# Warm-up multiplications, a first weight half in two pieces, and query tile before key tile in a two-layer block kernel

## The chip, the cores and the metric

One core of a Trainium2 chip runs the whole program. The metric is the device time in microseconds (us), the median of three runs. Engines: TensorE (PE; PEld is its weight load), VectorE (DVE), ScalarE (ACT), GpSimd (POOL), SyncE (SP, here only a queue that issues transfers).

## The reference, cut to what matters

A sequence of 256 tokens of width 1024 goes through two layers. Each layer normalises the tokens, multiplies them by the wide `w_in` and mixes them in four branches; the attention branch needs normalised queries and keys:

```python
xn = rms_norm(h, norm1_g[layer])
z = xn @ w_in[layer]
q, k, va = jnp.split(z[..., OFF_ATTN:OFF_GATE], 3, axis=-1)
q = rms_norm(q, q_g)                      # over 64 features, 8 groups
k = rms_norm(k, k_g)
bias = rel_bias[rel_buckets(qp, kp)]
logits = einsum('bhmqd,bhmkd->bhmqk', qb, kb) * scale + bias
```

Behind the mixing follow a dense feed-forward part in layer 0 and eight experts in layer 1, then a second block of two layers with other mixers. The change touches only the start of the program and the query and key part of both layers of the first block.

## The kernel before

Every product of a float32 activation with a float32 weight is made of three: high by high, low by high and high by low part, where high is the value rounded to the short format and low what is left. ACT makes the high part of a weight half (`split`, line 1672, 128x2048) and DVE the low part (line 2194). `weigh` takes the halves of a tile in turn: per half and token block it issues 4 x 2 matmuls with the high weights (alternating xT_high and xT_low) and then 4 with the low weights, all on line 917. A tile of 1024 x 512 (Q, K, V and so on) has two halves, so 24 matmuls for each of the two token blocks, 48 in all.

**Loads.** SP issues x block 0, x block 1 and then all weight halves in order of use (lines 838, 839, 836): Q, K and V have two halves of 1 MB each. Five raw slots hold halves, so the first five loads (Q both, K both, V first) wait for nothing; V's second half takes the slot of Q's first half and is asked for once PE has used it for both blocks. POOL issues 26 loads of constants; its large ones (line 1550, 2.8 MB with the masks in first_constants) wait until Q's second half is in.

**Token blocks.** Each block of 128 tokens is normalised (ACT line 1636 for the squares, lines 1626 and 1627 for the root, DVE line 2179), turned by 8 transposes on PE (`norm_turn`, line 964), and copied by ACT to xT_high (line 1643) and by DVE to xT_low (line 2187).

**Order on PE** in `mixer`: Q block 0, transposes of x block 1, K block 0, Q block 1, K block 1, each by `by_block`. In layer 0 the transposes of x block 0 come first; in layer 1 they come earlier, and the splits of Q and K lie in the feed-forward part before. Then come VEC (a small product for the bias, layer 0 only), SW (transposes of the gating weights), QT (transposes of the normalised queries, two blocks), V, KT (of the keys), UV with its two results U and SV, in layer 0 FLIP (line 1035), and A.

**Order on ACT and DVE.** Both run fixed lists. For the norm of each of Q and K, block by block: ACT squares the result (`head_squares`, line 1731), DVE sums (`head_sums`, line 2267), ACT takes the root in two steps (`head_roots`, lines 1626 and 1627), DVE multiplies (`head_norm`, line 2274). Between these steps lie the splits of V and UV. Behind them DVE copies VEC (line 2293), prepares parameters (line 2246 on) and masks SW (line 2302). POOL writes the copied VEC to DRAM (line 1554), reads it back shifted (line 1556) as `brev`, and PE waits for that before FLIP.

**Banks.** Results take eight PSUM banks in turn, in the order of `first_jobs`; `begin` waits until the job that had the bank eight jobs before has been drained. In layer 0 U has the bank of VEC and SV that of SW; in layer 1 U has that of K block 1 and SV that of SW. `weigh` asks for all banks of its jobs before its first matmul.

Of the kernel before, what the change touches and what calls it, by code (L numbers as in the profile page):

```python
# [60 lines left out]
NHIGH = 3  # L61

# [164 lines left out]
def first_jobs(l):  # L227
    j = norm_jobs("1", l, blocks=(0,)) if l == 0 else []
    j += [("Q", l, 0)] + norm_jobs("1", l, blocks=(1,)) + [("K", l, 0), ("Q", l, 1), ("K", l, 1)]
# [135 lines left out]
def kernel_program(nc, t):  # L365
# [28 lines left out]
    with ctx:  # L394
# [3 lines left out]
        def sem(name):  # L398
            return ctx.enter_context(nc.semaphore(name))
# [122 lines left out]
        lgt = A(2, 2, SEQ)  # L522
        prb = A(2, 2, SEQ)
# [123 lines left out]
        x_in, ident_in, first_in = sem("x_in"), sem("ident_in"), sem("first_in")  # L647
# [11 lines left out]
        rt_weights, rt_mask = sem("rt_weights"), sem("rt_mask")  # L659
        hn_y_out, index_ready, rows_fetched = sem("hn_y_out"), sem("index_ready"), sem("rows_fetched")  # L660
        sel_ready, f_sel_ready, moe_done, f_done = sem("sel_ready"), sem("f_sel_ready"), sem("moe_done"), sem("f_done")
        flag_ready, router_high_in = sem("flag_ready"), sem("router_high_in")
# [158 lines left out]
        def _(sp):  # L821
# [16 lines left out]
            sp.dma_start(h[:, 0, :], t["x"][0, 0:P, :]).then_inc(x_in, 16)  # L838
            sp.dma_start(h[:, 1, :], t["x"][0, P:SEQ, :]).then_inc(x1_in_out_done, 16)
            for half in DENSE[:FIRST_HALVES]:  # L840
                load_half(half)
# [39 lines left out]
        def _(pe):  # L881
# [121 lines left out]

            def mixer(l):
                if l == 0:
                    pe.wait_ge(ident_in, 16)
                    norm_turn(("1", l), 0, xs, (norm_x, 1))
                pe.wait_ge(*drained(("X", "1", l, 0, 1)))
                by_block(("Q", l), ("Q", l), 0)
                norm_turn(("1", l), 1, xs, (norm_x, 4 * l + 2))  # L1010
                by_block(("K", l), ("K", l), 0)
                pe.wait_ge(*drained(("X", "1", l, 1, 1)))
                by_block(("Q", l), ("Q", l), 1)
                by_block(("K", l), ("K", l), 1)
# [6 lines left out]
                def heads(name, src, first):  # L1021
                    for b in range(TB):
                        pe.wait_ge(qk_n, at(l, 4, 2 * b + first + 1))
# [261 lines left out]
            pe.wait_ge(rt_mask, 1)  # L1285
# [329 lines left out]
        def _(act):  # L1615
            steps = Steps(act, act_step)
            act.dma_start(norm1_row, t["norm1_g"][0].partition_broadcast(P)).then_inc(norm1_row_in[0], 16)
            act.dma_start(ident, t["common_constants"][:, 0:P]).then_inc(ident_in, 16)
# [99 lines left out]
            def mixer(l):  # L1718
                if l == 0:
                    log_exp()  # L1720
                    norm(0, (x_in, 16))
                    norm(1, (x1_in_out_done, 16))
                    high("1", l, 0)
                    split(("Q", l))
                    split(("K", l))
                    high("1", l, 1)
# [6 lines left out]
                def head_roots(n, b):  # L1733
                    k = 2 * n + b
                    act.wait_ge(qk_ss, at(l, 4, 2 * b + n + 1))
                    inv_root(tiny[:, 8 * k:8 * k + 8], tiny[:, 8 * k:8 * k + 8], QK, qk_r)
                head_squares(0, 0)
                head_squares(1, 0)
                head_roots(0, 0)
# [1325 lines left out]
```

## Time and profile before

| | |
|---|---|
| median of 3 runs | 2178.29 us (2177.87 to 2179.69) |
| the profiled execution | 2178.79 us, its span 2176.6 us |
| PE busy | 2137.2 us, 98% of the span, 10935 matmuls |
| DVE, ACT busy | 1591.8 us (73%), 1331.9 us (61%) |
| PE, share of the chain that ended last | 90%; DVE 4%, transfers 3%, ACT 2% |

The span runs from the first to the last instruction; the execution is 2.2 us longer. In a timeline a line gives the start, the duration, the engine and source line, the operation, how many were merged (x8), and, where the engine sat idle before, how long and which operation ended it. Matmuls overlap, so their spacing is less than the duration shown.

### The profile page before, as it was taken

What the parts mean: (1) busy time and instruction counts of PE and PEld (TensorE: products, weight loads), DVE (VectorE), ACT (ScalarE), POOL (GpSimd) and SP (SyncE); (2) the same over time, 40 slices, a digit from 0 to 9 for tenths busy, and PEclk for the clock granted to TensorE, in tenths of its full rate; (3) what the DMA queues carried; (4) which work ended last, traced back from release to release, by engine and by line L of the source; (5) the groups of instructions that cost most, each with busy time, mean ns of one, the idle gap of its engine ahead of it and who ended that gap; (6) DMA issues with size and microseconds to landing.
All of it is one profiled execution on the core that took longest, in us unless ns stands there. A gap on an engine that the chain in (4) does not pass through costs nothing.

```text
span 2176.6 us, 27831 instructions
## 1 busy us (share of the span) xinstructions
PE 2137.2 (98%) x10935; PEld 1811.7 (83%) x10935; DVE 1591.8 (73%) x1339; ACT 1331.9 (61%) x1151; POOL 78.2 (4%) x67
## 2 busy tenths in 40 slices
PE   7999999999998999999999999999999999999998
PEld 5988788888787888888888888888888898899987
DVE  5577555466766888888888889888896667565665
ACT  4475544355655777777777777777765545456542
POOL 3100000000000000000000000000110000000000
PEclk9999999999998999999999999999999999999999
DMA  8554565554548999999999999999996534455442
GB/s 281 157 190 150 206 199 184 178 187 149 194 153 294 351 373 380 375 380 375 389 370 386 379 378 373 383 382 373 388 368 218 174 124 148 163 179 170 132 155 78
DMA packets 249165, 569.70 MB, mean 262 GB/s; under 512 B 12168, under 2 KB 14352, under 8 KB 248816
## 3 DMA queue, kind: packets, MB, share of 16 engines
q1 hardware_dynamic: 242368, 546.41, 70.3%
q0 software_dynamic: 5136, 16.70, 2.3%
q10 hardware_dynamic: 1568, 5.31, 0.6%
q8 instruction: 64, 1.05, 0.2%
q14 instruction: 29, 0.24, 0.0%
HBM read 562.60 MB, written 5.78 MB: 261 GB/s over the span
## 4 chain that ended last, share of the span: by engine, by line
PE 90%; DVE 4%; DMA 3%; ACT 2%; issue 0%; SPq 0%; DVEq 0%; ACTq 0%
PE bank L917 33%; PE bank L1178 9%; PE bank L1179 9%; PE bank L1182 9%; PE bank L923 9%; PE bank L1226 5%; PE bank L1219 5%; PE bank L1221 5%; PE bank L964 3%; DMA ring<-w_in 2%; DVE halves_r L2194 1%; DMA ring<-moe_w_down 1%; ACT halves_r L1672 1%; DVE w_low L2622 0%; DMA ring<-w_out 0%
## 5 line engine op out<-in xcount | busy, mean ns | idle before, releaser
L2622 DVE TENSOR_TENSOR w_low<-ring,w_high 128x4096 fp32r<-128x4096 f32 x167 | 736.4, 4421 | 80.5 <-ACT w_high L1901 80.2
L1901 ACT ACTIVATE w_high<-ring 128x4096 fp32r<-128x4096 f32 x167 | 607.1, 3636 | 232.8 <-DMA ring<-moe_w_gate_up 137.0
L917 PE MATMUL bank<-halves_r,xT_high 128*128 128x512 f32 (+1 forms) x1856 | 562.6, 381 | 5.9 <-ACT halves_r L1672 3.2
L2194 DVE TENSOR_TENSOR halves_r<-ring,halves_r 128x2048 fp32r<-128x2048 f32 x175 | 391.4, 2264 | 160.9 <-ACT halves_r L1672 159.0
L917 PEld LDWEIGHTS bank<-halves_r,xT_high 128*128 128x128 f32 x1856 | 343.8, 189 | 73.1 <-issue 5.2
L1672 ACT ACTIVATE halves_r<-ring 128x2048 fp32r<-128x2048 f32 x175 | 326.2, 1892 | 118.6 <-DMA ring<-w_in 57.4
L1178 PE MATMUL bank<-w_high,xg_high 128*128 128x512 f32 x896 | 354.7, 396 | 1.7 <-DVE xg_low L2599 1.7
L1179 PE MATMUL bank<-w_high,xg_low 128*128 128x512 f32 x896 | 349.6, 390 | 0.0
L917 PE MATMUL bank<-halves_r,xT_low 128*128 128x512 f32 (+1 forms) x928 | 348.5, 380 | 0.0
L1182 PE MATMUL bank<-w_low,xg_high 128*128 128x512 f32 x896 | 221.6, 389 | 0.0
L917 PEld LDWEIGHTS bank<-halves_r,xT_low 128*128 128x128 f32 x928 | 175.3, 189 | 31.7
L1178 PEld LDWEIGHTS bank<-w_high,xg_high 128*128 128x128 f32 x896 | 168.4, 188 | 35.9 <-issue 1.9
L1182 PEld LDWEIGHTS bank<-w_low,xg_high 128*128 128x128 f32 x896 | 168.1, 188 | 35.1 <-DVE w_low L2622 0.2
L1179 PEld LDWEIGHTS bank<-w_high,xg_low 128*128 128x128 f32 x896 | 168.4, 188 | 33.8
L1219 PE MATMUL bank<-w_high,hid_high 128*128 128x512 f32 x448 | 176.5, 394 | 0.0
L1221 PE MATMUL bank<-w_high,hid_low 128*128 128x512 f32 x448 | 174.5, 390 | 0.0
L923 PE MATMUL bank<-xT_high,halves_r 128*128 128x256 f32 x896 | 165.2, 284 | 0.0
L1650 ACT ACTIVATE arena<-bank 128x512 f32<-128x512 f32 x82 | 47.4, 597 | 158.1 <-PE bank L923 82.8
L923 PEld LDWEIGHTS bank<-xT_high,halves_r 128*128 128x128 f32 x896 | 141.0, 192 | 0.9 <-issue 0.8
L1226 PE MATMUL bank<-w_low,hid_high 128*128 128x512 f32 x448 | 112.2, 389 | 0.6 <-DVE w_low L2622 0.6
L923 PE MATMUL bank<-xT_low,halves_r 128*128 128x256 f32 x448 | 108.8, 283 | 0.0
L1219 PEld LDWEIGHTS bank<-w_high,hid_high 128*128 128x128 f32 x448 | 84.1, 188 | 19.2 <-ACT w_high L1901 2.0
(392 smaller groups left out, 2310.9 us busy)
## 6 DMA issues: line engine op xcount, KB each, us to landing
ring<-moe_w_gate_up SPq DMA_DIRECT2D x224, 1024.0 KB, 10.6
ring<-moe_w_down SPq DMA_DIRECT2D x112, 1024.0 KB, 9.8
ring<-w_in SPq DMA_DIRECT2D x108, 1024.0 KB, 5.1
ring<-w_out SPq DMA_DIRECT2D x24, 1024.0 KB, 4.9
ring<-ffn_w_gate_up SPq DMA_DIRECT2D x22, 1024.0 KB, 5.2
ring<-ffn_w_down SPq DMA_DIRECT2D x11, 1024.0 KB, 4.9
ring<-w_mem_kv SPq DMA_DIRECT2D x8, 1024.0 KB, 5.2
ring<-w_branch_attn SPq DMA_DIRECT2D x4, 1024.0 KB, 5.1
```

What stands on the lines that cost most here:

```text
L917: return pe.matmul(o[:, a:a + n], x[:, c, b * P:(b + 1) * P], w[:, k, col:col + n], **flags)
L923: return pe.matmul(o[:, a:a + SEQ], w[:, k, j * P:(j + 1) * P], x[:, c, :], **flags)
L1178: pe.matmul(o[:, :], xg_high[:, c, :], w[:, c, :], start=c == 0, stop=False)
L1179: pe.matmul(o[:, :], xg_low[:, c, :], w[:, c, :], start=False, stop=False)
L1182: mm = pe.matmul(o[:, :], xg_high[:, c, :], w[:, c, :], start=False, stop=c == KC - 1)
L1219: pe.matmul(acc[n][:, :], hid_high[:, 4 * k + c, :], v[:, c, :], start=k + c == 0, stop=False)
L1221: pe.matmul(acc[n][:, :], hid_low[:, 4 * k + c, :], v[:, c, :], start=False, stop=False)
L1226: mm = pe.matmul(acc[n][:, :], hid_high[:, 4 * k + c, :], v[:, c, :], start=False, stop=4 * k + c == EX_CH - 1)
L1672: act.activation(top_view(half), raw_view(half), ACT.Copy).then_inc(top_in, 1)
L1901: act.activation(high_slot(k), ring[:, ring_r.slot(names[k]), :], ACT.Copy).then_inc(w_high_in[r], 1)
L2194: dve.tensor_tensor(raw_view(half, halves_r), raw_view(half), top_view(half).bitcast(F32), ALU.subtract).then_inc(raw_low_in, 1)
L2622: dve.tensor_tensor(w_low[:, slot, :], ring[:, slot, :], high_slot(k).bitcast(F32), ALU.subtract).then_inc(w_low_in[r], 1)
```

## The change

- SP loads Q's first half in two pieces of two chunks each: the first piece between x block 0 and x block 1, the second behind x block 1. ACT and DVE make its high and low parts piece by piece.
- DVE sets 640 columns to zero at the very start, and PE multiplies them 20 times (512 columns each) into a bank that nobody reads, before it waits for the identity matrix and the first piece, whose arrival the same semaphore now tells.
- In layer 0 `first_queries` replaces the block-wise order: Q's chunks 0 and 1 for block 0, chunks 2 and 3, the transposes of x block 1, the low part for block 0, the near half for block 1, then the far half for both blocks.
- In both layers the order is Q block 0, transposes, Q block 1, and then K for both blocks joined, half by half (in layer 0 behind `first_queries`). ACT's and DVE's lists are put in that order, root and norm directly behind their squares and sums; the two splits of UV now stand together behind the last root and norm.
- Some semaphores are shared by two uses (renamed, with higher counts).

The diff, cut to its core:

```diff
+WARM_UP = 20
...
-    j += [("Q", l, 0)] + norm_jobs("1", l, blocks=(1,)) + [("K", l, 0), ("Q", l, 1), ("K", l, 1)]
+    j += [("Q", l, 0)] + norm_jobs("1", l, blocks=(1,)) + [("Q", l, 1), ("K", l, 0), ("K", l, 1)]
...
+        zeros_r = rounded("zeros_r", [P + WIDE], arena_at + 4 * A.at)
...
+            first, first_from = raw_view(DENSE[0]), dense_source(*DENSE[0])
+            sp.dma_start(first[:, 0:2, :], first_from[:, 0:2, :]).then_inc(ident_piece_in, 16)
             sp.dma_start(h[:, 1, :], t["x"][0, P:SEQ, :]).then_inc(x1_in_out_done, 16)
-            for half in DENSE[:FIRST_HALVES]:
+            sp.dma_start(first[:, 2:4, :], first_from[:, 2:4, :]).then_inc(raw_full[raws.slot(DENSE[0])], 16)
+            for half in DENSE[1:FIRST_HALVES]:
...
+            def first_queries():
+
+                tile = ("Q", 0)
+                near, far = (tile, 0), (tile, 1)
+                out = {0: begin((*tile, 0))}
+
+                def high(b, w, c, k):
+                    rows(b)(out[b], xT_high, w, c, k, start=c == 0, stop=False)
+                    return rows(b)(out[b], xT_low, w, c, k, start=False, stop=False)
+
+                def low(b, w, c, k):
+                    return rows(b)(out[b], xT_high, w, c, k, start=False, stop=c == KC - 1)
+
+                pe.wait_ge(*drained(("X", "1", 0, 0, 0)))
+                pe.wait_ge(piece_top_router_high, 1)
+                for c in (0, 1):
+                    high(0, top_view(near), c, c)
+                w = high_half(near)
+                for c in (2, 3):
+                    high(0, w, c, c)
+                norm_turn(("1", 0), 1, xs, (norm_x, 2))
+                w_low = low_half(near)
+                for c in range(4):
+                    low(0, w_low, c, c)
+                out[1] = begin((*tile, 1))
+                pe.wait_ge(*drained(("X", "1", 0, 1, 0)))
+                for c in range(4):
+                    mm = high(1, w, c, c)
+                mm.then_inc(top_free[tops.slot(near)], 1)
+                for c in range(4):
+                    mm = low(1, w_low, c, c)
+                mm.then_inc(*raw_end(near))
+                pe.wait_ge(*drained(("X", "1", 0, 0, 1)))
+                pe.wait_ge(*drained(("X", "1", 0, 1, 1)))
+                w = high_half(far)
+                for b in range(TB):
+                    for k in range(4):
+                        mm = high(b, w, 4 + k, k)
+                mm.then_inc(top_free[tops.slot(far)], 1)
+                w_low = low_half(far)
+                for b in range(TB):
+                    for k in range(4):
+                        mm = low(b, w_low, 4 + k, k)
+                    mm.then_inc(*end((*tile, b)))
+
             def mixer(l):
                 if l == 0:
-                    pe.wait_ge(ident_in, 16)
+                    pe.wait_ge(zeros_rt_mask, 1)
+                    for k in range(WARM_UP):
+                        pe.matmul(bank[NBANK - 1][:, :], zeros_r[:, 0:P], zeros_r[:, P:P + WIDE], start=True, stop=True)
+                    pe.wait_ge(ident_piece_in, 32)
                     norm_turn(("1", l), 0, xs, (norm_x, 1))
-                pe.wait_ge(*drained(("X", "1", l, 0, 1)))
-                by_block(("Q", l), ("Q", l), 0)
-                norm_turn(("1", l), 1, xs, (norm_x, 4 * l + 2))
-                by_block(("K", l), ("K", l), 0)
-                pe.wait_ge(*drained(("X", "1", l, 1, 1)))
-                by_block(("Q", l), ("Q", l), 1)
-                by_block(("K", l), ("K", l), 1)
+                    first_queries()
+                else:
+                    pe.wait_ge(*drained(("X", "1", l, 0, 1)))
+                    by_block(("Q", l), ("Q", l), 0)
+                    norm_turn(("1", l), 1, xs, (norm_x, 4 * l + 2))
+                    pe.wait_ge(*drained(("X", "1", l, 1, 1)))
+                    by_block(("Q", l), ("Q", l), 1)
+                weigh(("K", l), [(("K", l, b), [rows(b)]) for b in range(TB)])
                 pe.wait_ge(first_in, FIRST_LOADS * 16)
                 if l == 0:
                     pe.matmul(begin(("VEC",))[0:MAPS, 0:REL], rel_tab, rel_hot, start=True,
...
-                        pe.wait_ge(qk_n, at(l, 4, 2 * b + first + 1))
+                        pe.wait_ge(qk_n, at(l, 4, 2 * first + b + 1))
...
                 if l == 0:
                     log_exp()
                     norm(0, (x_in, 16))
+                    first, first_top = raw_view(DENSE[0]), top_view(DENSE[0])
+                    act.wait_ge(ident_piece_in, 32)
+                    act.activation(first_top[:, 0:2, :], first[:, 0:2, :], ACT.Copy).then_inc(piece_top_router_high, 1)
+                    high("1", l, 0)
                     norm(1, (x1_in_out_done, 16))
-                    high("1", l, 0)
-                    split(("Q", l))
+                    act.wait_ge(raw_full[raws.slot(DENSE[0])], 16)
+                    act.activation(first_top[:, 2:4, :], first[:, 2:4, :], ACT.Copy).then_inc(top_in, 1)
+                    high("1", l, 1)
+                    split(("Q", l), (1,))
                     split(("K", l))
-                    high("1", l, 1)

                 def head_squares(n, b):
                     job = ("QK"[n], l, b)
...
-                    act.wait_ge(qk_ss, at(l, 4, 2 * b + n + 1))
+                    act.wait_ge(qk_ss, at(l, 4, k + 1))
                     inv_root(tiny[:, 8 * k:8 * k + 8], tiny[:, 8 * k:8 * k + 8], QK, qk_r)
                 head_squares(0, 0)
+                head_roots(0, 0)
+                head_squares(0, 1)
+                head_roots(0, 1)
+                split(("V", l), (0,))
                 head_squares(1, 0)
-                head_roots(0, 0)
                 head_roots(1, 0)
-                split(("V", l), (0,))
-                head_squares(0, 1)
                 split(("V", l), (1,))
-                head_roots(0, 1)
                 head_squares(1, 1)
-                split(("UV", l), (0,))
                 head_roots(1, 1)
-                split(("UV", l), (1,))
+                split(("UV", l))
                 act.wait_ge(first_in, 16 * FIRST_LOADS)
                 act.wait_ge(par_exp, 2 * l + 1)
                 act.activation(small[:, l, 16:18], small[:, l, 14:16], ACT.Exp).then_inc(par_exp, 1)
...

             def mixer(l):
                 if l == 0:
+                    dve.memset(zeros_r[:, :].bitcast(F32), 0.0).then_inc(zeros_rt_mask, 1)
+                    first, first_top, first_low = raw_view(DENSE[0]), top_view(DENSE[0]), raw_view(DENSE[0], halves_r)
                     dve.wait_ge(norm1_row_in[0], 16)
-                    for b in range(TB):
-                        norm(b, b + 1, norm1_row)
+                    norm(0, 1, norm1_row)
+                    dve.wait_ge(piece_top_router_high, 1)
+                    dve.tensor_tensor(first_low[:, 0:2, :], first[:, 0:2, :], first_top[:, 0:2, :].bitcast(F32),
+                                      ALU.subtract)
                     lower("1", l, 0)
-                    split(("Q", l))
+                    norm(1, 2, norm1_row)
+                    dve.wait_ge(top_in, 1)
+                    dve.tensor_tensor(first_low[:, 2:4, :], first[:, 2:4, :], first_top[:, 2:4, :].bitcast(F32),
+                                      ALU.subtract).then_inc(raw_low_in, 1)
+                    lower("1", l, 1)
+                    split(("Q", l), (1,))
                     split(("K", l))
-                    lower("1", l, 1)

                 def head_sums(n, b):
                     k = 2 * n + b
-                    dve.wait_ge(qk_sq, at(l, 4, 2 * b + n + 1))
+                    dve.wait_ge(qk_sq, at(l, 4, k + 1))
                     dve.tensor_reduce(tiny[:, 8 * k:8 * k + 8], shaped(sq_t[:, k, :], 8, QK), AX.X,
                                       ALU.add).then_inc(qk_ss, 1)

                 def head_norm(n, b):
                     job, dst = ("QK"[n], l, b), (q_n, k_n)[n]
                     k = 2 * n + b
-                    dve.wait_ge(qk_r, at(l, 4, 2 * b + n + 1))
+                    dve.wait_ge(qk_r, at(l, 4, k + 1))
                     link(dve.tensor_tensor(shaped(dst[:, b, :], 8, QK), shaped(out_of(job)[:, :], 8, QK),
                                            over(tiny[:, 8 * k:8 * k + 8], QK), ALU.mult))
                     dve.sem_inc(qk_n, 1)
                     dve.sem_inc(*fr(job))
                 head_sums(0, 0)
+                head_norm(0, 0)
+                head_sums(0, 1)
+                head_norm(0, 1)
+                split(("V", l), (0,))
                 head_sums(1, 0)
-                head_norm(0, 0)
                 head_norm(1, 0)
-                split(("V", l), (0,))
-                head_sums(0, 1)
                 split(("V", l), (1,))
-                head_norm(0, 1)
                 head_sums(1, 1)
-                split(("UV", l), (0,))
                 head_norm(1, 1)
-                split(("UV", l), (1,))
+                split(("UV", l))
                 if l == 0:
                     dve.wait_ge(first_in, 16 * FIRST_LOADS)
                     dve.wait_ge(*full(("VEC",)))
```

## Rows read from the trace of the kernel before

**Rows 1.** Busy time by stretches: us, PE, PEld, DVE, ACT, POOL, PEclk, DMA, GB/s.

```profile
66.33:100.00 33.67, 33.67 (x259) 31.32 (x258) 18.95 (x29) 13.59 (x13) 7.26 (x10) 1.00 0.57 143
...
1644.00:1648.00 4.00, 3.79 (x21) 3.71 (x20) 0.00 (x0) 3.97 (x4) 0.00 (x0) 0.62 0.60 225
```

**Rows 2.** Timeline of ACT, layer 0: start us, us, engine, line, operation, [idle before, releaser].

```profile
6.22 1.06 ACT L1636 ACTIVATE xs<-h 128x1024 f32<-128x1024 f32 x1 [3.25 <-DMA h<-x]
...
8.35 1.06 ACT L1636 ACTIVATE xs<-h 128x1024 f32<-128x1024 f32 x1 [0.51 <-DMA h<-x]
...
12.45 1.91 ACT L1672 ACTIVATE halves_r<-ring 128x2048 fp32r<-128x2048 f32 x1 [0.50 <-DMA ring<-w_in]
16.54 1.91 ACT L1672 ACTIVATE halves_r<-ring 128x2048 fp32r<-128x2048 f32 x1 [2.19 <-DMA ring<-w_in]
...
33.20 1.92 ACT L1672 ACTIVATE halves_r<-ring 128x2048 fp32r<-128x2048 f32 x1 [2.04 <-DMA ring<-w_in]
...
43.44 0.21 ACT L1627 ACTIVATE arena<-arena 128x8 f32<-128x8 f32 x1
```

**Rows 3.** Timeline of all engines, 9 to 12 us.

```profile
9.38 1.94 PE L964 MATMUL bank<-consts,xs 128*128 128x128 f32 x8 [9.38 <-DVE xs L2179]
...
10.01 1.28 DVE L2179 SCALAR_TENSOR_TENSOR xs<-h,rstd,arena 128x1024 f32<-128x1024 f32 x1 [0.77 <-ACT rstd L1627]
...
11.21 1.47 DVE L2187 TENSOR_TENSOR xT_low<-bank,xT_high 128x512 fp32r<-128x512 f32 x2
```

**Rows 4.** Timeline of DVE, layer 0, 35 to 51 us.

```profile
35.15 2.29 DVE L2194 TENSOR_TENSOR halves_r<-ring,halves_r 128x2048 fp32r<-128x2048 f32 x1 [2.94 <-ACT halves_r L1672]
...
41.55 0.68 DVE L2274 TENSOR_TENSOR arena<-bank,arena 128x512 f32<-128x512 f32 x1
42.48 0.69 DVE L2267 TENSOR_REDUCE arena<-arena 128x8 f32<-128x512 f32 x1 [0.24 <-DVE arena L2274]
43.08 2.28 DVE L2194 TENSOR_TENSOR halves_r<-ring,halves_r 128x2048 fp32r<-128x2048 f32 x1
...
48.42 0.54 DVE L2293 COPY arena<-bank 8x384 f32<-8x384 f32 x1
...
50.57 0.69 DVE L2302 TENSOR_TENSOR arena<-bank,consts 128x512 f32<-128x512 f32 x1
```

**Rows 5.** Timelines of PE and of POOL, layer 0, 40 to 66 us.

```profile
40.43 0.81 PE L1017 MATMUL bank<-arena 32*8 32x384 f32 x2
...
54.57 0.36 PE L923 MATMUL bank<-xT_high,halves_r 128*128 128x256 f32 x1
...
66.17 1.03 PE L1035 MATMUL bank<-arena,consts 128*128 128x256 f32 x4
...
49.25 0.55 POOL L1554 DMA_DIRECT2D bias_by_distance<-arena  x1 [26.32 <-DVE arena L2293]
...
63.45 0.90 POOL L1570 DMA_DIRECT2D par_all<-mem_norm_g  x1 [8.47 <-DMA arena<-bias_by_distance]
```

**Rows 6.** Timelines of PE and of DVE, layer 1, 442 to 474 us.

```profile
442.00 1.03 PE L964 MATMUL bank<-consts,xs 128*128 128x128 f32 x8
...
461.65 0.66 PE L964 MATMUL bank<-consts,arena 128*128 128x128 f32 x4 [1.40 <-DVEq L2276]
...
473.87 0.36 PE L923 MATMUL bank<-xT_high,halves_r 128*128 128x256 f32 x1
...
443.29 1.28 DVE L2187 TENSOR_TENSOR xT_low<-bank,xT_high 128x512 fp32r<-128x512 f32 x2
...
467.98 0.15 DVE L2246 SCALAR_TENSOR_TENSOR arena<-arena 128x1 f32<-128x1 f32 x1
...
469.69 0.69 DVE L2302 TENSOR_TENSOR arena<-bank,consts 128x512 f32<-128x512 f32 x1
```

**Rows 7.** Chain of work that ended last, layer 1: start us, us, what.

```profile
462.31 10.93 PE bank L917 x48
```

**Rows 8.** Timeline of PE, behind the experts.

```profile
1642.71 0.35 PE L923 MATMUL bank<-mg_high_a,halves_r 128*128 128x256 f32 x1 [2.23 <-DVE mg_low_b L2708]
```

More of the change, by code:

```diff
@@ L646, in kernel_program @@
         f_bank_free = [sem(f"f_bank_free{k}") for k in range(NBANK)]
-        x_in, ident_in, first_in = sem("x_in"), sem("ident_in"), sem("first_in")
+        x_in, ident_piece_in, first_in = sem("x_in"), sem("ident_piece_in"), sem("first_in")
         vec_out, brev_in = sem("vec_out"), sem("brev_in")
@@ L658, in kernel_program @@
         merged_up = sem("merged_up")
-        rt_weights, rt_mask = sem("rt_weights"), sem("rt_mask")
+        rt_weights, zeros_rt_mask = sem("rt_weights"), sem("zeros_rt_mask")
         hn_y_out, index_ready, rows_fetched = sem("hn_y_out"), sem("index_ready"), sem("rows_fetched")
         sel_ready, f_sel_ready, moe_done, f_done = sem("sel_ready"), sem("f_sel_ready"), sem("moe_done"), sem("f_done")
-        flag_ready, router_high_in = sem("flag_ready"), sem("router_high_in")
+        flag_ready, piece_top_router_high = sem("flag_ready"), sem("piece_top_router_high")
         ye_high_in = {"m": sem("ye_high_in"), "f": sem("f_ye_high_in")}
@@ L1284, in _ @@
                 norm_turn(("E",), b, memS, (mem_x, b + 1))
-            pe.wait_ge(rt_mask, 1)
+            pe.wait_ge(zeros_rt_mask, 2)
             o = begin(("RK",))
@@ L1617, in _ @@
             act.dma_start(norm1_row, t["norm1_g"][0].partition_broadcast(P)).then_inc(norm1_row_in[0], 16)
-            act.dma_start(ident, t["common_constants"][:, 0:P]).then_inc(ident_in, 16)
+            act.dma_start(ident, t["common_constants"][:, 0:P]).then_inc(ident_piece_in, 16)
             def log_exp():
@@ L1958, in _ @@
             mixer(0)
-            act.activation(flat(router_high), flat(router), ACT.Copy).then_inc(router_high_in, 1)
+            act.activation(flat(router_high), flat(router), ACT.Copy).then_inc(piece_top_router_high, 1)
             ffn()
@@ L2508, in route @@
                                            over(index[:, :, k], 8), ALU.is_equal))
-                dve.tensor_tensor(chosen_r, rt[:, 72:88], rt[:, 88:104], ALU.add).then_inc(rt_mask, 1)
+                dve.tensor_tensor(chosen_r, rt[:, 72:88], rt[:, 88:104], ALU.add).then_inc(zeros_rt_mask, 1)
                 top = shaped(rt[:, 16:32], TB, 8)
@@ L2513, in route @@
                 dve.wait_ge(*full(("RK",)))
-                dve.wait_ge(rt_mask, 1)
+                dve.wait_ge(zeros_rt_mask, 2)
                 link(dve.scalar_tensor_tensor(out=pos[:, :, 0:8], in0=shaped(out_of(("RK",))[:, 0:16], TB, 8), scalar=1.0,
@@ L2695, in _ @@
             mixer(0)
-            dve.wait_ge(router_high_in, 1)
+            dve.wait_ge(piece_top_router_high, 2)
             dve.tensor_tensor(flat(router_low), flat(router), flat(router_high).bitcast(F32), ALU.subtract)
```

## The prediction

> **What bounds the kernel now.** I read three views in this order. First the page (table above): TensorE (PE) is busy 98% of the span, nearly all of it matmuls that the change keeps, so only its idle time can be won. Then the busy time by stretches: after the first 66 us PE is busy without a gap [rows 1], so whatever moves the start of the FLIP matmuls, at 66.17 us [rows 5], moves the end by as much. Then the timelines of the first 66 us, engine by engine, because all that the change touches lies there and in the same stretch of layer 1, 442 to 474 us.
>
> In the first 66 us three clocks run beside each other. The loads: x block 0 is in at 6.2, x block 1 at 8.35, the first half of the Q weights at 12.45, the second at 16.54, and the first half of V only at 33.20, because GpSimd's large constant loads start once Q's second half is in and share the transfer engines [rows 2]. PE: 8 transposes take 1.94 us at 9.38 and 1.03 at 442.00 [rows 3, 6], the two levels of 1.2 and 2.4 GHz; at the upper one 48 matmuls of 512 columns take 10.93 us, 0.228 each [rows 7]. VectorE (DVE): from 35.15 on it has one long list, low parts of V and UV, sums and norms of Q and K, the copy of VEC, the masking of SW [rows 4]. The reader should see that this list, not PE, decides what a faster start is worth.
>
> **The start: zeros, split load, first_queries.** The SP queue now holds x0, first piece, x1, second piece; the bytes are the same. x1 came 2.1 us after x0 and has 512 KB; the 1 MB of Q's first half came 4.1 after x1 [rows 2]. So the first piece is in at 8.4, x1 at 10.4, the second piece at 12.45, and what is behind keeps its time.
>
> The Trainium skill ("DMA: Bandwidth & Descriptors", Anatomy of one DMA) gives each DMA about 2 us of fixed cost beside its bytes. Paid in series by the one extra DMA it would make every later load, V's too, 2.0 us later and put the estimate 2.0 us higher. The rows speak against it: 512 KB and 1 MB arrive at the same rate, with no room for a fixed part between queued DMAs.
>
> The memset and the 20 multiplications of zeros run on engines that have nothing to do before x is in. At twice 0.228 they last at most 9.1 us, so they may hold the first transposes (9.38, rows 3) by up to 1.3 us.
> Then, with the rows' durations: ACT splits the first piece at 8.7 to 9.8 (half of a split) and copies the transposes of x0 to 11.2; norm 1 follows there and not at 8.35, so that DVE has x1's norm (1.66 from ACT's start, then 1.28, rows 2, 3) at 14.3 instead of 11.3. DVE has the piece's low part at 11.1 and the first low transpose at 11.8; there PE begins Q block 0, with 4 matmuls. It waits for the second piece's top (13.95), does 4 more, the 8 transposes of x1, 4 low ones, waits for block 1's first low transpose (17.1), does 12, and from 19.8, behind the split of Q's second half, the last 24. Q is done for both blocks at 25.3. K, joined, is 48 matmuls: 36.2, its block 0, after 44 of them, 35.3. K's loads are early enough. VEC (0.74), SW and both QT (12 transposes, 1.2), V (10.93) and KT (0.8) bring PE to UV at 49.9, where it was at 54.57 [rows 5]. If nothing else were late, the start would give 4.7 us.
>
> **What is late next.** UV's accumulators reuse the banks of VEC and SW, which DVE drains behind its whole list. VEC also feeds the bias round trip through DRAM that FLIP waits for. So DVE's list in the new order:
> - V's first half is in at 33.20 as before: its load is queued from the start, and GpSimd's loads begin when they did. Low part 35.15 to 37.4 [rows 4]. K block 0 and its squares (36.2) are not late.
> - Sum from 37.36; from its start to the end of ACT's roots were 1.17 us (42.48 to 43.65, rows 4, 2): 38.53. The norm holds DVE 0.93 (41.55 to 42.48, rows 4), to 39.5.
> - ACT's split of V's second half is now behind these roots: 38.45 to 40.35. Its load, which ended this wait before, is asked for much earlier, when Q block 1 has used the near half. Low part from 40.4; it holds DVE 2.2: 42.6.
> - Sum, roots to 43.75, norm to 44.7. ACT's split of UV, behind the roots too, ends at 45.57. Low parts of UV from 45.6 and 47.8; the VEC copy starts at 50.0.
>
> Before, it started at 48.42 [rows 4]: now 1.6 later, although PE is 4.7 earlier. The splits of UV used to fill the time in which DVE waited for the roots; now these waits are open. SW's masking starts 2.15 behind the copy and takes 0.69 [rows 4]: banks free at 52.85. PE starts UV at 52.9 and has waited 3.0 us, a wait that was not there, with everything behind it. FLIP is ready 11.6 later (54.57 to 66.17, rows 5): 64.5. The bias round trip ends at 63.45 before [rows 5]; 1.6 later, PE has it at about 64.85 (POOL sees it 0.2 late). FLIP starts at 64.85 instead of 66.17: **layer 0 gains 1.3 us** of the 4.7. Bounds: 4.7 gained, if the list is not the limit; and 1.7 lost, if the round trip, 14.2 us now [rows 5], takes a fifth longer (67.8), since 2.7 of slack are all it had.
>
> **Layer 1, where there is no start to win.** The same code orders layer 1.
> - Q block 1 now follows block 0 directly and needs x1's low transposes, which K block 0 covered. PE ends the transposes at about 442.8, DVE ends the low ones at 443.29 + 1.28 = 444.57 [rows 6]: PE loses 1.8.
> - 72 matmuls (Q block 1, K) take 16.4: SW at 461.0. The wait of 1.40 before QT block 1 [rows 6] goes, since Q's norms are long done. V starts at 462.2, against 462.1. By PE alone UV starts at 473.9, against 473.87 [rows 6]: nothing won or lost.
> - But K block 0 is done at 460.2 instead of 448. Sum from 460.9, roots 462.1, V's second half on ACT to 464.0 and on DVE to 466.15, sum and roots to 467.3, UV on ACT to 469.1, on DVE from 469.15 and 471.35 to 473.6. The parameter steps start at 473.6 instead of 467.98, SW's masking 1.71 later, and takes 0.69 [rows 6]: 476.0. PE starts UV at 476.0: **layer 1 loses 2.1 us**, with 0 (the list is quicker) and 3 as bounds.
>
> **Sum.** The profiled execution has 2178.79 us, its span 2176.6 and 2.2 around it. -1.3 + 2.1 = +0.8: 2179.6. The median of the runs is 0.5 lower: **2179.1**. That is within 0.2% (4.4 us, about what a measurement of this kernel can tell from no change).
>
> **Rivals.**
> - A: the start reaches the end. For it: PE alone is at UV at 49.9. Against it: V's first half is tied to 33.20 and the list behind it is in a fixed order. Layer 0 -4.7, layer 1 +2.1: 2175.7. If the list does not bind in layer 1 either, 2173.6, just faster by over 0.2%.
> - B: slower, through the clock. The change makes PE wait 3.0 us before UV in layer 0, 1.8 before Q block 1 and 2.1 before UV in layer 1. In the old trace a wait of 2.23 at 1642.71 [rows 8] was followed by a stretch whose granted clock is 0.62 in the mean of 4 us, the lower level most of the time [rows 1]; the wait of 1.40 [rows 6] was not. It decides between these. Price: 0.38 x 4 = 1.5 us and a little before it, 1.6. In layer 0 the first 0.35 of it is covered by the round trip. Once: 2180.5; three times: 2183.5, slower. The Trainium skill ("TensorE: Matmul & The Clock Gate", Loop structure matters more than you think) holds that matmuls behind long waits run cold; the rows at 1642.71 agree. By that rule all three new waits would cost it, and the time would be this rival's 2183.5.
> - C: the zeros don't do what they are there for: the clock falls again behind them. 12 matmuls more at 0.456 cost Q up to 2.5 us; the sum over K block 0 can start 1.2 late before DVE waits for it; 1.3 of it shows: 2180.4.
>
> **How the numbers follow.** The forecast 0.52; A 0.17 (0.05 of it at 2173.6); B 0.22 (0.08 of it slower by over 0.2%); C 0.09. The range leaves out the far ends of A and B: 2174.8 to 2183.2. Faster by over 0.2%: 0.05, slower: 0.08, within: 0.87.
>
> **What would show it.** Right: the VEC copy near 50.0, UV starting near 52.9 released by DVE, FLIP near 64.9; in layer 1 PE idle at 443 to 444.6 and before UV, not before QT block 1. Wrong: PE goes into UV without a wait (A); a clock below 1 near 53, 445 or 476 (B); transposes or matmuls at the lower level past 18 us (C); V's first half not in at 33.2, which would move all of layer 0.

## The result, and the profile after

| | before | changed |
|---|---|---|
| median, 8 runs each | 2178.60 us (2177.38 to 2181.13) | 2184.53 us (2182.47 to 2186.17) |
| ratio | | 1.0021, 95% interval 1.0012 to 1.0031 |
| the profiled execution, span | 2178.79, 2176.6 us | 2182.55, 2180.7 us |

The change costs time: 5.9 us by the medians; the ratio on record, which is not the quotient of the medians, gives 4.6 us, its interval 2.6 to 6.8. The forecast was 2179.1, made of a loss of 0.8 us, with a range to 2183.2. The median lies 1.3 above that range; by the ratio the time beside the forecast's own base (2178.29) would be 2182.9, just inside it. Three executions, 2609 us of the kernel before and 3249 and 5971 us of the kernel before with zeros, are far slower than all others and count in no ratio and in no median below.

The page of the changed kernel (busy us, share, instructions):

```profile
span 2180.7 us, 27881 instructions
## 1 busy us (share of the span) xinstructions
PE 2144.0 (98%) x10955; PEld 1816.5 (83%) x10955; DVE 1592.5 (73%) x1341; ACT 1331.2 (61%) x1152; POOL 78.2 (4%) x67
```

PE has only 20 matmuls more, the zeros, and 6.8 us more of busy time. Where the time went can be read by four milestones that both kernels have. The first two are where the change is. This is DVE's timeline in layer 0 of the changed kernel (start us, us, engine, line, operation), beside [rows 4]:

```profile
35.16 2.29 DVE L2252 TENSOR_TENSOR halves_r<-ring,halves_r 128x2048 fp32r<-128x2048 f32 x1 [3.03 <-ACT halves_r L1726]
...
38.56 0.69 DVE L2340 TENSOR_TENSOR arena<-bank,arena 128x512 f32<-128x512 f32 x1 [0.52 <-ACT arena L1681]
40.37 2.29 DVE L2252 TENSOR_TENSOR halves_r<-ring,halves_r 128x2048 fp32r<-128x2048 f32 x1 [1.11 <-ACT halves_r L1726]
42.57 0.68 DVE L2333 TENSOR_REDUCE arena<-arena 128x8 f32<-128x512 f32 x1
...
45.58 4.50 DVE L2252 TENSOR_TENSOR halves_r<-ring,halves_r 128x2048 fp32r<-128x2048 f32 x2 [1.12 <-ACT halves_r L1726]
49.99 0.54 DVE L2358 COPY arena<-bank 8x384 f32<-8x384 f32 x1
...
52.14 0.69 DVE L2367 TENSOR_TENSOR arena<-bank,consts 128x512 f32<-128x512 f32 x1
```

PE and POOL, beside [rows 5]:

```profile
52.93 0.35 PE L928 MATMUL bank<-xT_high,halves_r 128*128 128x256 f32 x1 [1.45 <-issue]
...
64.51 1.68 PE L1089 MATMUL bank<-arena,consts 128*128 128x256 f32 x7
...
50.82 0.55 POOL L1608 DMA_DIRECT2D bias_by_distance<-arena  x1 [27.73 <-DVE arena L2358]
...
62.63 0.90 POOL L1624 DMA_DIRECT2D par_all<-mem_norm_g  x1 [5.72 <-DMA arena<-bias_by_distance]
```

DVE's list came out as forecast: V's low part at 35.16, then two waits of 0.52 and 1.11 us for the roots and for ACT's split (38.56, 40.37), the sum of K block 1 at 42.57, the same two waits again before UV's low parts at 45.58, the VEC copy at 49.99 (forecast 50.0) although before it was at 48.42. PE starts UV at 52.93 (52.9), but its wait before it is 1.45 us and not the forecast 3.0: PE itself comes to UV at 51.48 and not at 49.9. FLIP, the matmuls behind UV that use the bias, starts at 64.51 instead of 66.17: layer 0 gains 1.7 us.

Layer 1, PE and DVE, beside [rows 6]:

```profile
442.94 0.50 PE L922 MATMUL bank<-halves_r,xT_high 128*128 128x512 f32 x1 [1.59 <-DVE xT_low L2245]
...
474.49 0.35 PE L928 MATMUL bank<-xT_high,halves_r 128*128 128x256 f32 x1 [1.77 <-issue]
...
464.58 0.68 DVE L2333 TENSOR_REDUCE arena<-arena 128x8 f32<-128x512 f32 x1
...
473.70 0.69 DVE L2367 TENSOR_TENSOR arena<-bank,consts 128x512 f32<-128x512 f32 x1
```

PE waits 1.59 us before Q block 1 and 1.77 before UV, which DVE releases with SW's masking (473.70) and which starts at 474.49 instead of 473.87. From a lead of 1.66 us the kernel goes to arrears of 0.62: layer 1 loses 2.3 us. So far the sum of the forecast (+0.8) stands at +0.6.

The other milestones lie behind the experts, where the source is the same in both. PE there in the changed kernel:

```profile
1642.69 0.55 PE L928 MATMUL bank<-mg_high_a,halves_r 128*128 128x256 f32 x1 [2.66 <-DVE mg_low_b L2773]
...
1644.54 0.41 PE L928 MATMUL bank<-mg_high_a,halves_r 128*128 128x256 f32 x1
1648.12 0.58 PE L928 MATMUL bank<-mg_low_a,halves_r 128*128 128x256 f32 x1 [3.17 <-issue]
...
1652.82 0.40 PE L1210 MATMUL bank<-ye_high,selT 128*128 128x512 f32 x1
```

and before:

```profile
1648.36 0.27 PE L923 MATMUL bank<-mg_high_a,halves_r 128*128 128x256 f32 x1 [0.57 <-issue]
...
1648.83 0.40 PE L1156 MATMUL bank<-ye_high,selT 128*128 128x512 f32 x1
```

The matmuls behind the wait for mg_low_b start at 1642.69 now and at 1642.71 before [rows 8]: level. The scatter behind them (L1210, L1156 before) starts at 1652.82 now and 1648.83 before: 4.0 us lost within 6 us of work. Now PE issues 9 matmuls, the last at 1644.54, and then stops for 3.17 us; before it issued 28 and stopped for 0.57. The trace names no releaser ("issue"). And the clock, by stretches (us, PE, PEld, DVE, ACT, POOL, PEclk, DMA, GB/s), now

```profile
664.00:684.00 20.00, 16.21 (x102) 15.48 (x101) 12.53 (x34) 8.94 (x14) 0.00 (x0) 0.74 0.96 345
1640.00:1656.00 16.00, 10.18 (x53) 9.55 (x53) 4.90 (x10) 9.92 (x10) 0.00 (x0) 0.68 0.39 146
```

and before

```profile
664.00:684.00 20.00, 16.22 (x94) 15.56 (x92) 12.06 (x32) 8.83 (x13) 0.00 (x0) 0.66 0.95 344
1640.00:1656.00 16.00, 13.20 (x88) 12.39 (x87) 8.74 (x14) 12.93 (x18) 0.00 (x0) 0.89 0.54 192
```

is 0.68 instead of 0.89 in these 16 us (PEclk, the granted clock). At the start of the experts (664 to 684 us) it is the other way, 0.74 against 0.66, and that makes up the 0.6 us of arrears; this mean differs between the kernels' profiled executions, from 0.51 to 0.74. Of the 4.0 us, 2.6 are the longer stop (3.17 - 0.57); the rest, 1.4, I put down to the clock. Behind the scatter both take 527.8 us to the end.

### The profile page after: what moved, and what is told of

Its sections match the earlier page's. It is cut to its first block, busy times and chain, and to the rows that moved or that the text cites. A ratio compares the mean times of both kernels' runs of the same rounds, so it can differ in the third digit from the quotient of the medians.

```text
span 2180.7 us, 27881 instructions
## 1 busy us (share of the span) xinstructions
PE 2144.0 (98%) x10955; PEld 1816.5 (83%) x10955; DVE 1592.5 (73%) x1341; ACT 1331.2 (61%) x1152; POOL 78.2 (4%) x67
## 4 chain that ended last, share of the span: by engine, by line
PE 91%; DVE 4%; DMA 2%; ACT 1%; issue 1%; DVEq 0%; SPq 0%; ACTq 0%
PE bank L922 34%; PE bank L1232 9%; PE bank L1233 9%; PE bank L1236 9%; PE bank L928 9%; PE bank L1280 5%; PE bank L1273 5%; PE bank L1275 5%; PE bank L969 3%; DVE halves_r L2252 1%; DMA ring<-moe_w_down 1%; ACT halves_r L1726 1%; DMA ring<-w_in 0%; DMA h<-x 0%; DVE w_low L2687 0%
```

## The experiments

I had two theories. CODE: the stop behind 1644.54 is PE waiting for its next instructions, and its place depends on how many instructions lie ahead of it in the program; the 20 zeros moved it. CLOCK: the loss is a stretch at the lower clock level that happens to fall there. Unless said otherwise the ratios are to the kernel before on the same chip.

**Without the zeros.** `WARM_UP = 0` in the changed kernel.

> The changed kernel without the 20 multiplications of zeros (only the memset and its wait stay). Theory CODE: of the 5.9 us that the change costs, 0.6 come from layers 0 and 1 (-1.7 in layer 0, +2.3 in layer 1) and the rest from behind the experts, where PE stops after 9 matmuls at 1644.5 and waits 3.2 us for nothing that the trace names; I take that for the arrival of its next instructions, and the 20 zeros shift the place of the stop by 20 matmuls. So here PE runs about 29 matmuls there before it stops, the stop is under 1 us, and the time is 2179 to 2181. Theory CLOCK: the loss is the lower clock level behind 1642, which comes from when the stretch falls; as the start before 33 us is hidden by V's load, nothing moves, and the time stays at 2184 to 2185 with the stop after 9 matmuls. Both: DVE's VEC copy stays within 0.3 of 50.0 and UV within 0.3 of 52.9 (K block 0 gets later by up to 2 us, and DVE waits for it only from 37.4 on).

Measured 2180.91 us, ratio 1.0006 (0.9997 to 1.0014). PE behind the experts, and the VEC copy:

```profile
1646.70 0.55 PE L928 MATMUL bank<-mg_high_a,halves_r 128*128 128x256 f32 x1 [2.40 <-DVE mg_low_b L2773]
...
1652.11 0.39 PE L928 MATMUL bank<-mg_low_a,halves_r 128*128 128x256 f32 x1 [0.20 <-issue]
```

```profile
50.87 0.54 DVE L2358 COPY arena<-bank 8x384 f32<-8x384 f32 x1
```

The stop is 0.20 us instead of 3.17, and it ends 5.4 us after PE went on, as in the changed kernel (1642.69 to 1648.12). Only now PE had work for nearly all of this time: 29 matmuls. The place moved by the 20 matmuls taken out, as CODE says and CLOCK does not. The VEC copy is 0.9 late, outside what I had written: without the zeros the transposes and the first Q matmuls run at the lower level, and K block 0 gets late enough for DVE.

**With 32 zeros.** `WARM_UP = 32`.

> The changed kernel with 32 multiplications of zeros instead of 20. They end near 12 us, hidden as far as UV is concerned. Theory CODE: the stop moves by another 12 matmuls, from 9 behind the wait for mg_low_b to before it; there it is either hidden in that wait or a full stretch of instructions is at hand behind it, so no stop of over 1 us stands among the first 30 matmuls, and the time is 2178 to 2181. Theory CLOCK: no difference to the changed kernel, 2184 to 2185.

Measured 2177.89 us, ratio 0.9989 (0.9980 to 0.9998): against the changed kernel's 1.0021 some 7 us less, for 12 useless multiplications more. Behind the experts:

```profile
1645.24 0.55 PE L928 MATMUL bank<-mg_high_a,halves_r 128*128 128x256 f32 x1 [3.41 <-DVE mg_low_b L2773]
```

There is no stop behind this row. The wait for mg_low_b is 3.41 instead of 2.66 us: the stop seems to have moved into it, with about 1 us of it left. DVE starts on mg_low_b 2.1 us before PE goes on here, 0.8 to 1.4 us before in the twelve traces other than this one and narrow12's (2.2).

**The kernel before with the zeros.**

```diff
+                    pe.wait_ge(zeros_rt_mask, 1)
+                    for k in range(WARM_UP):
+                        pe.matmul(bank[NBANK - 1][:, :], zeros_r[:, 0:P], zeros_r[:, P:P + WIDE], start=True, stop=True)
                     pe.wait_ge(ident_in, 16)
```

> The kernel before with only the memset and the 20 multiplications of zeros added ahead of the identity wait. They end near 9.0 us, before the transposes can begin, and Q block 0 may gain up to 0.8 us by the higher clock, which V's load hides. Theory CODE: the stop behind the experts moves from 28 to about 8 matmuls and lasts 3 us or more, the clock falls for longer there, and the time is 3 to 6 us over the kernel before: 2181.5 to 2184.5. Theory CLOCK: nothing moves behind 33 us, the time is that of the kernel before within 1 us.

Measured 2183.19 us, ratio 1.0012 (1.0003 to 1.0021).

```profile
1645.09 0.35 PE L925 MATMUL bank<-mg_high_a,halves_r 128*128 128x256 f32 x1 [2.21 <-DVE mg_low_b L2714]
...
1650.92 0.37 PE L925 MATMUL bank<-mg_high_a,halves_r 128*128 128x256 f32 x1 [4.64 <-issue]
```

The first 66 us hardly differ (FLIP 65.92 instead of 66.17). The stop is 4.64 us, after 8 matmuls, and from the wait's end to the scatter PE takes 9.9 us instead of 6.1. That is the loss that the zeros cause there; in this execution PE was also 2.4 us later at the wait (1645.09, before 1642.71), after a granted clock of 0.58 from 664 to 684 us.

**The same with narrow zeros,** `bank[...][:, 0:32]` and 32 columns instead of 512.

> The kernel before with 20 multiplications of zeros of 32 columns each instead of 512: the same number of PE instructions as in old_plus_zeros, next to no work and no warmer clock. Theory CODE: the stop behind the experts comes after 8 matmuls as there, and the time is 2 to 5 us over the kernel before. Rival (the 20 wide multiplications cost by the work or by the clock they set going): the stop is after 28 matmuls, the time that of the kernel before.

Measured 2182.19 us, ratio 1.0018 (1.0009 to 1.0027).

```profile
1645.69 0.36 PE L925 MATMUL bank<-mg_high_a,halves_r 128*128 128x256 f32 x1 [2.16 <-DVE mg_low_b L2714]
...
1651.51 0.37 PE L925 MATMUL bank<-mg_high_a,halves_r 128*128 128x256 f32 x1 [4.25 <-issue]
```

As many instructions, a sixteenth of the columns, the same stop of over 4 us. It is the number, not the work.

**The lists woven as before.** On ACT and DVE, for roots read norm:

```diff
                 head_squares(1, 0)
-                head_roots(1, 0)
                 split(("V", l), (1,))
+                head_roots(1, 0)
                 head_squares(1, 1)
+                split(("UV", l), (0,))
                 head_roots(1, 1)
-                split(("UV", l))
+                split(("UV", l), (1,))
```

> The changed kernel with the lists of ACT and DVE woven as before: V's second split before the root and norm of K block 0, UV's first split before the root and norm of K block 1, its second behind; PE's order is untouched. My theory of the open waits for the roots: the VEC copy starts near 48.2 instead of 50.0, UV in layer 0 starts at 51.5 (PE's own arrival), in layer 1 about 1.8 earlier than 474.49 in distance from its Q, so 3.2 us less than the changed kernel up to layer 1, and 2181 by the median if what is behind the experts is unchanged (PE's instructions are the same in number). Rival: the lists are bound by DVE's busy time alone, and weaving wins under 0.5 us.

Measured 2182.36 us, ratio 1.0009 (1.0000 to 1.0018). PE in layer 0, and all that it waits for from 430 to 480 us:

```profile
51.38 0.36 PE L928 MATMUL bank<-xT_high,halves_r 128*128 128x256 f32 x1 [1.07 <-issue]
...
62.97 1.24 PE L1089 MATMUL bank<-arena,consts 128*128 128x256 f32 x5
```

```profile
PE bank L922 <- DVE xT_low L2246: 1.6, 1, 1.6
```

FLIP starts at 62.97, 1.5 us before the changed kernel, and the wait before UV of layer 1 is gone; only the one before Q block 1 is left. The waits for the roots were open, and closing them is worth what I had put (3.2 us forecast; 1.5 in layer 0 and, from Q block 1 to UV, 1.8 in layer 1). The stop behind the experts is there as before, 3.17 us after 9 matmuls, and so the median stays over that of the kernel before.

**Layer 1 in the old order.**

```diff
-                    pe.wait_ge(*drained(("X", "1", l, 1, 1)))
-                    by_block(("Q", l), ("Q", l), 1)
-                weigh(("K", l), [(("K", l, b), [rows(b)]) for b in range(TB)])
+                    by_block(("K", l), ("K", l), 0)
+                    pe.wait_ge(*drained(("X", "1", l, 1, 1)))
+                    by_block(("Q", l), ("Q", l), 1)
+                    by_block(("K", l), ("K", l), 1)
+                if l == 0:
+                    weigh(("K", l), [(("K", l, b), [rows(b)]) for b in range(TB)])
```

> The changed kernel with layer 1 in the order of before (Q block 0, transposes, K block 0, Q block 1, K block 1, lists of ACT and DVE woven as before); layer 0 is the changed one. My theory: the 2.3 us that layer 1 loses come back (no wait before Q block 1, the 1.4 us before QT block 1 again, UV without a wait), UV of layer 1 starts 1.7 us before its 473.87 of before, and the median is 2.3 under the changed kernel's, near 2182.2, with the stop behind the experts after 5 to 9 matmuls, since PE has a few waits more. Rival: layer 1's loss is a following of layer 0's and stays.

Measured 2180.34 us, ratio 1.0012 (1.0003 to 1.0021). PE's only wait from 430 to 480 us, before QT block 1:

```profile
PE bank L970 <- DVEq L2360: 1.0, 1, 1.0
```

The lead of layer 0 (FLIP at 64.43) goes through layer 1 undiminished: UV starts at 471.78, 2.1 us before its 473.87. The loss there is layer 1's own. The stop behind the experts is 3.63 us after 8 matmuls:

```profile
1638.78 0.55 PE L929 MATMUL bank<-mg_high_a,halves_r 128*128 128x256 f32 x1 [2.07 <-DVE mg_low_b L2805]
...
1644.46 0.37 PE L929 MATMUL bank<-mg_high_a,halves_r 128*128 128x256 f32 x1 [3.63 <-issue]
```

**The start undone.** Whole halves, and in `mixer` for layer 0 too:

```diff
-                    first_queries()
+                pe.wait_ge(*drained(("X", "1", l, 0, 1)))
+                by_block(("Q", l), ("Q", l), 0)
+                norm_turn(("1", l), 1, xs, (norm_x, 4 * l + 2))
+                pe.wait_ge(*drained(("X", "1", l, 1, 1)))
+                by_block(("Q", l), ("Q", l), 1)
```

> The changed kernel without the pieces and without first_queries: whole halves, Q block 0, transposes, Q block 1, K joined; zeros and lists stay. My theory: DVE's list is tied to V's load only as long as K block 0 is done by 36.2; here it is done near 39.3, so the list starts 2 to 3 us later, the VEC copy is near 52.5, UV of layer 0 near 55.5, FLIP near 67, 2.5 us later than in the changed kernel, and the median 2.5 above it (2187). Rival: the start is hidden altogether by V's load at 33.2, then UV stays at 52.9 and the time at 2184.5.

Measured 2187.02 us, ratio 1.0042 (1.0028 to 1.0055). DVE and PE:

```profile
41.34 0.69 DVE L2316 TENSOR_REDUCE arena<-arena 128x8 f32<-128x512 f32 x1 [3.55 <-ACT arena L1780]
...
53.97 0.54 DVE L2341 COPY arena<-bank 8x384 f32<-8x384 f32 x1
```

```profile
56.92 0.36 PE L925 MATMUL bank<-xT_high,halves_r 128*128 128x256 f32 x1 [1.34 <-issue]
```

DVE waits 3.55 us for K block 0's squares (L2316 at 41.34 instead of 37.37), the VEC copy is 4.0 us later, UV too. The direction is as forecast, but the delay in layer 0 is 4.0 and not 2.5; that the median is the forecast one to the microsecond is luck. Behind the experts PE stops for 4.41 us after 9 matmuls. The joined order needs the quick start; it is not hidden altogether.

**Putting it together.** The woven lists, layer 1 in the old order, and behind the 20 wide multiplications 24 narrow ones.

> All that the runs so far point to together: the changed start in layer 0, the woven lists, layer 1 in the old order, and 24 narrow multiplications (32 columns) behind the 20 wide ones, so that the place where PE waits for its instructions falls before the wait for mg_low_b. My theory: FLIP starts 3.1 us before its 66.17, layer 1 keeps that, no stop of over 1 us behind 1640, and the median is 2.5 to 4 us under the kernel before (2175 to 2176). Rival: the clock levels behind 665 and 1642 take the gain back, and the time is within 1 us of the kernel before.

Measured 2173.83 us, ratio 0.9978 (0.9969 to 0.9987): faster than both kernels, and with no stop behind mg_low_b. The gain is 4.6 us by the medians, more than the 2.5 to 4 expected, although FLIP came at 64.27, 1.9 and not 3.1 us before 66.17: the narrow ones end at 10.8 us and hold the transposes (10.64, in the changed kernel 9.27), and from 12 to 18 us the granted clock is 0.52.

**The changed kernel once more, and two kernels with narrow zeros first.**

> The changed kernel itself, beside the next two on one chip. 4 to 6 us over the kernel before; the stop of about 3 us after 9 matmuls behind the experts.

Measured 2184.10 us, ratio 1.0022 (1.0013 to 1.0032), a stop of 3.50 us after 9 matmuls. This execution shows one more thing. PE, and the clock of 50 to 56 us:

```profile
53.13 0.36 PE L928 MATMUL bank<-xT_high,halves_r 128*128 128x256 f32 x1 [2.84 <-issue]
...
53.59 0.42 PE L928 MATMUL bank<-xT_low,halves_r 128*128 128x256 f32 x1
...
50.00:56.00 6.00, 3.16 (x18) 2.95 (x17) 5.11 (x12) 4.28 (x5) 1.47 (x2) 0.79 0.54 181
```

After 2.84 us of idle time before UV the granted clock is 0.79 in the mean of 6 us, a single matmul of 256 columns goes from 0.28 us (in the first profiled execution) to 0.42, and FLIP starts at 66.20 instead of 64.51. In the first profiled execution the wait at this place was only 1.45 us and was not followed by it. PE came to UV later there, 51.48 instead of 50.29, since it had run at 0.50 from 14 to 16 us; here the clock was 1.00 from 12 to 18.

> The changed kernel with 12 narrow multiplications of zeros (32 columns) ahead of the 20 wide ones: the PE instruction count of zeros32, with next to no work added. Theory CODE: no stop after the wait for mg_low_b behind the experts, and a median 4 us or more under the changed kernel's. Rival (zeros32 was faster because the clock is kept up by more work): as the changed kernel.

Measured 2177.90 us, ratio 0.9992 (0.9983 to 1.0001), like 32 wide ones: no stop behind the wait for mg_low_b, and the wait itself as long as there.

```profile
1646.15 0.36 PE L929 MATMUL bank<-mg_high_a,halves_r 128*128 128x256 f32 x1 [3.44 <-DVE mg_low_b L2776]
```

> As woven_narrow with the 24 narrow multiplications ahead of the 20 wide ones instead of behind. In woven_narrow the clock was at its lower level from 12.3 to 19.1 us and FLIP started at 64.27, 1.3 later than in the kernel with woven lists alone (62.97). My theory: the narrow ones behind the wide ones let the clock fall longer; with them ahead FLIP starts at 63.0 to 63.4 and the median is 0.5 to 1 us below woven_narrow's. Rival: the length of that stretch is a matter of chance, and nothing changes beyond the spread.

Measured 2175.03 us, ratio 0.9981 (0.9972 to 0.9990), no gain over the other placing, and FLIP at 66.69, the opposite of what I expected. PE at the start:

```profile
1.60 5.30 PE L1060 MATMUL bank<-zeros_r 128*128 128x32 f32 x24 [1.60 <-DVE zeros_r L2336]
6.74 6.89 PE L1062 MATMUL bank<-zeros_r 128*128 128x512 f32 x20
```

24 multiplications of 32 columns took 5.3 us, 0.22 each, half of the 0.43 us by which the first ten wide ones behind them follow each other. Narrow zeros are no cheap filling; both placings hold the start.

**Instructions that are never run.** Lists and layer 1 as in the kernel put together, 20 wide zeros, and in PE's branch for an overflow of the experts, which these inputs never enter:

```diff
             with pe.If(more > 0):
-                pe.wait_ge(moe_done, 1)
+                for k in range(NOT_RUN):
+                    pe.wait_ge(moe_done, 1)
```

with `NOT_RUN = 49`.

> Woven lists, layer 1 in the old order, 20 wide multiplications of zeros, none narrow; instead 48 more waits on a semaphore in PE's branch for an overflow of the experts, which is never entered with these inputs, so that they take no time at all. Theory CODE in its form 'place in the program': the instructions behind the branch lie 48 places further, as in woven_narrow, so no stop of over 1 us behind mg_low_b; and as nothing holds the start, FLIP is near 63.0 (64.7 if the clock falls once), the median 5 to 7 us under the kernel before. Rival, 'number of instructions that PE has executed': the stop is back after about 8 matmuls, and the median is 0 to 2 us under the kernel before.

Measured 2173.16 us, ratio 0.9973 (0.9962 to 0.9984), 11 us under the changed kernel.

```profile
62.83 3.62 PE L1094 MATMUL bank<-arena,consts 128*128 128x256 f32 x16
...
1638.18 0.35 PE L930 MATMUL bank<-mg_high_a,halves_r 128*128 128x256 f32 x1 [2.23 <-DVE mg_low_b L2809]
```

FLIP is at 62.83, and no stop follows the wait for mg_low_b. Forty-eight instructions that never run have moved it. The run to hold beside it is layer1_old: PE's program there is the same but for these 48 waits, and it stops for 3.63 us. So what counts is the place in the program, not what PE has executed.

What is shown: the place of the stop moves with instructions put ahead of it, run or not, wide or narrow, and with it about 3 to 6 us. From the end of the wait for mg_low_b to the scatter PE takes 9.9 to 10.9 us in the seven traces with a stop after 8 or 9 matmuls, and 3.9 to 6.5 us in the seven others. What is argued: that PE waits there for the instructions behind the skipped branch. It fits that the stop ends 5.4 to 5.8 us after PE goes on in every kernel that has it (1648.12 - 1642.69, 1650.92 - 1645.09, 1651.51 - 1645.69), whatever it did meanwhile, and that a transfer of the instruction queue falls into it (1644 to 1648.4 us of the changed kernel; queue, kind: packets, MB, share):

```profile
q8 instruction: 1, 0.02, 1.5%
```

The packet runs from 1645.72 to 1646.77, and PE goes on 1.35 us after its end. In all nine traces with a stop one packet of this queue ends so, 1.35 to 1.60 us before PE goes on. With 32 wide or 12 narrow zeros more there is one that ends 1.7 us before the end of the lengthened wait (1643.56 and 1645.24 with 32 zeros). That ties the two closely; that PE waits for this transfer was still not shown, since no run moved the transfer alone.

## Why the prediction was right in two parts and wrong in the sum

- **The loads and the start.** Right: V's first half (33.21), so that no load behind the extra one came later, and the pieces. x1 was 0.7 us late (11.1, forecast 10.4), which ACT's work ahead of it hid. From 14 to 16 us the granted clock was 0.50, behind a wait of 1.13 us for the second piece, which is rival C in small. PE came to UV at 51.48 instead of 49.9, so the forecast wait of 3.0 us was mis-sized (1.45); in after_again, with the clock at 1.00 there, it was 2.84. K block 0's squares ended at 37.2 instead of 36.2, just in time for DVE at 37.37. start_old and zeros0 show how near that was: with the start undone the list is 4.0 late, without the zeros 0.9.
- **What is late next.** Right, to 0.1 us at each row of DVE's list and at the start of UV. `lists` shows the cause: the open waits for the roots.
- **The bias round trip.** The term was too long: 50.82 to 62.63, 11.8 us instead of the 14.2 taken from before. It was no limit, FLIP followed UV at 64.51, and layer 0 gained 1.7, not 1.3.
- **Layer 1.** Right: 1.59 before Q block 1 (forecast 1.8), no wait before QT block 1, 1.77 before UV (2.1), 2.3 lost in all (2.1).
- **The step that failed** is the first one: "whatever moves the start of the FLIP matmuls ... moves the end by as much". It took the program behind 66 us to be the same. Its source is; its place in the program is not, and behind the skipped branch that place decides when PE stops: 0.6 us of arrears up to layer 1, made up by 1642.7, became 4.0 at 1652.82. That the time by the ratio is still just inside the range is luck; the sum put nothing there. I had the row before me without reading it: 0.57 us of "issue" at 1648.36, the tail of the same wait, nearly hidden behind 28 matmuls. No term of the sum asked what 20 more instructions do besides running.
- **Rival B** gave the nearest number (2183.5), mostly for another reason. Its mechanism exists in one of the two profiled executions: in after_again 2.84 us of waiting before UV were followed by the lower level, and FLIP came 1.7 us later, near the price of 1.6. But not every new wait costs it: 1.45, 1.59 and 1.77 us were not followed by it. The main stretch at the lower level lies around the stop (granted clock 0.59 from 1640 to 1652, before 0.86); that the stop made it longer is likely, but was not shown apart.
- The step from the profiled execution (+3.8) to the medians (+5.9, and 4.1 beside after_again) is not split up. The 1.7 us of after_again, whose profiled execution of 2184.54 us has the time of the first median, may be part of it; how many executions have it is open.

## What to carry to other kernels

A faster start is worth only what the next list leaves of it: write out the list of the engine that drains the banks, in its new order, before counting PE's lead. Where two engines hand small results to and fro, keep a large independent piece between the question and the answer; that alone was worth 3.3 us in the trace here. And look for idle time of PE without a releaser behind a branch: here its place moved with instructions added at the start of the program and with some added inside the branch that was not taken. So compare edits only with that place held, or put it where PE waits anyway.

## What the runs showed that I had not expected

- A stop of PE of up to 4.6 us behind the experts, 5.4 to 5.8 us after it goes on, whose cost is set by how many matmuls lie before the place (29 without zeros: 0.20 us; 28 in the kernel before: 0.57; 8 or 9: 3.2 to 4.6; moved just ahead of the wait, by 12 instructions: about 1 us of it left in the wait; moved by 24 or 48: none seen).
- A multiplication of 32 columns took 0.22 us at the start of the program, half of the 0.43 us of one of 512 columns at the same pace, not a sixteenth; later, behind the wide ones of woven_narrow, 24 took 2.75 us, 0.115 each, again half of 0.228.
- An idle time of 2.84 us of PE (after_again) was followed by the lower clock level; 1.45 us before the same matmuls in the other profiled execution (UV at 52.93) were not. FLIP came at 66.20 in the one and at 64.51 in the other.
